# A DiT backbone on one core: the modulation's products change sides on TensorE

## What is computed

```python
def adaln_params(cond, w, b):
    mod = (jax.nn.silu(cond) @ w + b)[:, None, :]
    return jnp.split(mod, 6, axis=-1)
...
sh1, sc1, g1, sh2, sc2, g2 = adaln_params(c, ada_w[i], ada_b[i])
a = rms_norm(h, norm_g[i, 0]) * (1.0 + sc1) + sh1
```

## Time and profile before

| | |
|---|---|
| median of 3 runs | 3562.78 us (3562.68 to 3563.37) |
| the profiled execution | 3563.18 us |
| its span, first to last instruction | 3561.2 us |
| granted TensorE clock, mean | 0.91 |
| PE busy | 3002.9 us (84%) |
| DVE busy | 2108.3 us (59%) |

### The profile page before, as it was taken

How to read it: one execution, slowest core, us unless ns; L and a number is a source line. 1 busy time by engine, 2 the same in 40 slices (tenths; PEclk the granted TensorE clock), 3 DMA queues, 4 the chain that set the end, 5 groups by cost and what they waited for, 6 DMA issues and landing times.

```text
span 3561.2 us, 53031 instructions
## 1 busy us (share of the span) xinstructions
PE 3002.9 (84%) x20336; PEld 2752.0 (77%) x20336; DVE 2108.3 (59%) x2904; ACT 1211.9 (34%) x1744; POOL 140.0 (4%) x176
## 2 busy tenths in 40 slices
PE   7994882775998998899997768989875998989996
PEld 4772761664998998898997666767675998989996
DVE  3996998456535555645655246656446555664655
ACT  3113112333323243223341335656433333432332
POOL 0000000000000000000000001222100000000000
PEclk9996986887999999999998689999997999999998
DMA  6441430110222121122221110000021222223222
GB/s 239 170 142 45 132 106 12 42 48 30 77 71 71 65 77 65 60 71 71 71 89 57 38 48 25 1 1 1 24 71 41 89 89 78 95 78 106 91 93 77
DMA packets 69270, 254.28 MB, mean 71 GB/s; under 512 B 6672, under 2 KB 6928, under 8 KB 67984
## 3 DMA queue, kind: packets, MB, share of 16 engines
q1 hardware_dynamic: 54976, 202.60, 16.8%
q0 software_dynamic: 10880, 41.95, 3.6%
q10 hardware_dynamic: 3280, 7.86, 0.6%
HBM read 248.19 MB, written 4.19 MB: 71 GB/s over the span
## 4 chain that ended last, share of the span: by engine, by line
PE 65%; DVE 18%; issue 9%; ACT 7%; DVEq 1%; DMA 1%; POOL 0%; SPq 0%; ACTq 0%
PE PS L1165 54%; PE PS L1346 4%; DVE c L924 2%; PE PS L1333 2%; DVE w_lo L758 2%; DVE dw_acc L927 2%; DVE t L764 2%; DVE h L843 1%; DVE rms L768 1%; PE PS L1319 1%; PE PS L1174 1%; ACT t L427 1%; ACT a_hi L454 1%; PE PS L1320 1%; ACT prob L739 1%
## 5 line engine op out<-in xcount | busy, mean ns | idle before, releaser
L1165 PE MATMUL PS<-a_hi,w_hi 128*128 128x320 f32 (+4 forms) x4032 | 914.8, 309 | 245.6 <-DVE a_lo L802 157.5
L1165 PE MATMUL PS<-a_lo,w_hi 128*128 128x320 f32 (+4 forms) x4032 | 901.3, 306 | 0.0
L1165 PE MATMUL PS<-a_hi,w_lo 128*128 128x320 f32 (+4 forms) x4032 | 896.3, 305 | 0.0
L1165 PEld LDWEIGHTS PS<-a_hi,w_hi 128*128 128x128 f32 x4032 | 684.0, 198 | 261.9 <-DVE a_lo L802 163.1
L1165 PEld LDWEIGHTS PS<-a_lo,w_hi 128*128 128x128 f32 x4032 | 685.4, 198 | 0.0
L1165 PEld LDWEIGHTS PS<-a_hi,w_lo 128*128 128x128 f32 x4032 | 682.7, 198 | 0.0
L758 DVE TENSOR_TENSOR w_lo<-raw,w_hi 128x1024 fp32r<-128x1024 f32 x364 | 442.2, 1220 | 390.1 <-ACT w_hi L413 383.8
L413 ACT ACTIVATE w_hi<-raw 128x1024 fp32r<-128x1024 f32 x364 | 382.0, 1050 | 2.7 <-DVE y L1036 1.4
L1165 PE MATMUL PS<-z_hi,w_hi 128*128 128x320 f32 (+1 forms) x1408 | 309.1, 301 | 22.3 <-DVE z_lo L969 15.7
L1165 PE MATMUL PS<-z_lo,w_hi 128*128 128x320 f32 (+1 forms) x1408 | 304.7, 298 | 0.0
L1165 PE MATMUL PS<-z_hi,w_lo 128*128 128x320 f32 (+1 forms) x1408 | 304.3, 298 | 0.0
(11 more groups left out here) (160 smaller groups left out, 3525.0 us busy)
## 6 DMA issues: line engine op xcount, KB each, us to landing
raw<-wstream SPq DMA_DIRECT2D x364, 512.0 KB, 3.3
z<-adastream POOLq DMA_DIRECT2D x24, 1024.0 KB, 6.2
c<-adastream POOLq DMA_DIRECT2D x16, 1024.0 KB, 7.9
ada_first<-adastream SPq DMA_DIRECT2D x4, 2048.0 KB, 20.2
h<-xT SPq DMA_DIRECT2D x1, 2560.0 KB, 15.0
h<-xT ACTq DMA_DIRECT2D x1, 2560.0 KB, 11.9
out<-h ACTq DMA_DIRECT2D x1, 2048.0 KB, 9.5
out<-h ACTq DMA_DIRECT2D x2, 1024.0 KB, 4.3
```

The costliest lines, as they stand in the source:

```text
L1165: last = MM(PS[:, 2 * j + m, 0:n], wt[:, j, k, :], mv[:, k, m * n:(m + 1) * n], start=(k == 0 and p_ == 0), stop=(k == tiles - 1 and p_ == 2))
```

## The change

The operands change sides. A 128 x 128 block of the modulation's weights is now the stationary operand and `silu_c[:, k, :]` (128 x 2) the moving one; eight such matmuls sum straight into the 128 x 2 columns in PSUM that the turns used to write. The rows in PSUM, the copies of them by ACT, the tile `ada_row` and the turns go, with the semaphores `row_ready` and `ada_turned`. A group is 16 matmuls of the program. The sums move from PSUM bank 5 to bank 6. DVE's addition of the bias waits for `ada_used` in place of `ada_turned`.

```diff
-            return PS[:, 5, ds(512 - 4 * N_MOD + 2 * tile, 2 * n)]
+            return PS[:, 6, ds(512 - 4 * N_MOD + 2 * tile, 2 * n)]
...
-            def ada_rows_out(g):
-
-                act.wait_ge(ada_used, g + 1)
-                if above_zero(g - 1):
-                    act.wait_ge(ada_turned, g - 1)
-                A(ada_row[:, g % 2], PS[0:2, 6 + g % 2, 0:2 * P], ACT.Copy).then_inc(row_ready, 1)
...
-                        for r in range(x["ada_per"]):
-                            g = x["ada"] + x["ada_per"] * i + r
-                            act.wait_ge(ada_used, g + 1)
-                            act.wait_ge(ada_turned, g - 1 if r else g)
-                            A(ada_row[:, r % 2], PS[0:2, 6 + r % 2, 0:2 * P], ACT.Copy).then_inc(row_ready, 1)
...
-                dve.wait_ge(ada_turned, x["used"])
+                dve.wait_ge(ada_used, x["used"])
...
-            def ada_rows(g, weights, b):
-
-                for k in range(KT):
-                    last = MM(PS[0:2, 6 + b, 0:2 * P], silu_c[:, k, :], weights[:, k, :], start=(k == 0), stop=(k == KT - 1))
+            def ada_columns(g, weights):
+
+                for r in range(2):
+                    for k in range(KT):
+                        last = MM(ada_sums(2 * g + r, 1), weights[:, k, r * P:(r + 1) * P], silu_c[:, k, :],
+                                  start=(k == 0), stop=(k == KT - 1))
                 last.then_inc(ada_used, 1)
-
-            def ada_turn(g, b):
-
-                pe.wait_ge(row_ready, g + 1)
-                for r in range(2):
-                    last = MM(ada_sums(2 * g + r, 1), ada_row[:, b, r * P:(r + 1) * P], ident[0:2, 0:2], start=True, stop=True)
-                last.then_inc(ada_turned, 1)
...
-                        if above_zero(g - 1):
-                            pe.wait_ge(row_ready, g - 1)
-                        ada_rows(g, ada_first[:, g], g % 2)
-                        if g == ADA_FIRST // 2:
-                            pe.wait_ge(norm_step, x["pre"]["s"] + 6)
-                        if g:
-                            ada_turn(g - 1, (g - 1) % 2)
+                        ada_columns(g, ada_first[:, g])
                         if g == ADA_FIRST // 2 - 1:
                             average(x["pre"]["s"] + 4, wide_ap(x["pre"]["t"], x["pre"]["w"])[:, 0], x["pre"]["w"])
-                    ada_turn(ADA_FIRST - 1, (ADA_FIRST - 1) % 2)
...
-                            if r > 1:
-                                pe.wait_ge(row_ready, g - 1)
-                            ada_rows(g, slot_r, r % 2)
-                            if r:
-                                ada_turn(g - 1, (r - 1) % 2)
-                        ada_turn(x["ada"] + x["ada_per"] * (i + 1) - 1, (x["ada_per"] - 1) % 2)
+                            ada_columns(g, slot_r)
```

More of the change, by code:

```diff
@@ L200, in backbone @@
         dw_acc = sb("dw_acc", [P, CC - 640 + PAD], F32, rF + 2 * 2592)
-        ada_row = sb("ada_row", [2, 2, 2 * P], F32, rF + 2 * 2592 + 2688)
-        assert (CC - 640 + PAD) * 4 <= 2688 and 2 * 2592 + 2688 + 2048 <= 4 * 2592
+        assert (CC - 640 + PAD) * 4 <= 2 * 2592
         raw = sb("raw", [P, 2, KT, P], F32, rW)
@@ L253, in backbone @@
         ada_used, mod_ready, cond_ready = sem("ada_used"), sem("mod_ready"), sem("cond_ready")
-        row_ready, ada_turned = sem("row_ready"), sem("ada_turned")
         const_loaded, rope_loaded = sem("const_loaded"), sem("rope_loaded")
@@ L502, in _ @@
                 if kind == "pre":
-                    if "mod" in x:
-                        ada_rows_out(0)
                     pre_squares(x)
-                    if "mod" in x:
-                        for g in range(1, ADA_FIRST // 2):
-                            ada_rows_out(g)
                     root(s + 5, w)
                     if "mod" in x:
[L511 to L515, removed]
+                        split(0, 0)
+                        split(0, 1)
                         act.dma_start(h[:, :, 640:TOK], xT[:, :, 640:TOK]).then_inc(h_loaded[1], 16)
```

## The result

The changed kernel takes 3620.35 us (median of 4 runs, 3609.09 to 3621.34) against 3562.73: 57.6 us more, a ratio of 1.0159 with a 95% interval of 1.0142 to 1.0177. The profiled execution is the fastest of the four, 3609.09 us; the other three lie within 1.0 us of each other at 3620 to 3621.

A forecast was written before the change was run, and what follows sets the result against it. It took TensorE's modulation groups to bound the start and DVE both stages; 19.3 us in the start, 42 in stage A and 0 in stage B, on the profiled 3563.2, gave 3624 us in the median, range 3600 to 3646.

The forecast's parts named there:

- The bounds of before: Stages: DVE bounds both, at 27.54 us a pair in A (TensorE 26.76) and 29.06 in B (TensorE busy 23.98).
- The price of a record: Modulation groups: a 128-column load with its two-column matmul costs 0.111 us at full clock, 0.2135 at half.
- The rival in which a record costs 0.111 at either clock: Whole kernel: the clock falls but loads don't slow; start gains 3 us, 3560, not slower; chance 0.03.
- The clock: TensorE: never rises in the start; in stage A falls 3.8 us behind the units, needs 5.0 to return.
- The rival that it holds under loads: Whole kernel: loads keep the clock up, start gains at most 3.8 us, 3559, not slower; chance 0.07.
- The start: Eight groups at 6.83 us put DVE's addition of the bias at 68.5 instead of 49.17, 19.3 us later.
- Stage A: TensorE's pair takes 33.5 us against DVE's 27.54 and becomes the bound; seven times 6.0, 42 us.
- Two cases of the earlier trace: Full clock held 1.9 or 5.4 us behind wide matmuls; used to bound stage A's loss at 28 to 58 us.
- Stage B: TensorE's pair takes 26.7 us, under DVE's 29.06, so DVE stays the bound and the loss is 0.
- The sum: Whole kernel: 19.3 + 42 = 61.3 us on the profiled 3563.2, 3624 in the median.
- the signs named ahead: Trace: clock 0.50 to some 87 us, records 0.21 apart, units 33 to 34 apart, seven DVE waits of some 6 us.

The follow-up runs named there:

- the two parts of the stages: Kernel before with the operands swapped only in stage A: 3597.95 us against 3559.22; only in stage B: 3557.84 against 3559.34.
- the run in which 28 of 96 records a pair were worth all of the loss: Kernel before with stage A alone swapped, each pair's third group multiplying one of eight input tiles (sums incomplete): 3559.96 us against 3559.34.
- the wide forms: Changed kernel with the moving operand repeated to 128, 96, 64 or 32 columns: 3554.50 (again 3556.51), 3556.48, 3568.94 and 3604.33 us.
- the two profiles: Changed kernel, nothing altered, profiled in its first measurement (3609.1 us) and in a repeat on another chip (3616.4 us; median 3616.88 against 3558.67).

## Why the prediction was right

- **The bounds of before.** DVE in both stages, with TensorE 0.8 us behind in A: shown by the two parts of the stages (38.7 us in A, none in B) and by the run in which 28 of 96 records a pair were worth all of the loss.
- **The price of a record.** 0.2135 at half clock was taken from the 128-column records around those of the earlier trace rows (the 0.43 us shown there would give 0.215); measured 0.213. 0.111 at full clock was taken from the turns' loads of two rows; measured 0.112 with two moving columns and 0.111 with 128. The rival in which a record costs 0.111 at either clock (3560) is out. What the Trainium skill says in "TensorE: Matmul & The Clock Gate", section "LDWEIGHTS (loading the stationary operand)", a load's columns over 1.2 GHz, an estimated 107 ns for 128, fits the full clock alone; at half clock a record with its load takes 0.213 us, twice that, and the measurement decides.
- **The clock.** It stayed low for the whole start and fell in every pair of stage A. The rival that it holds under loads (3559) is refuted by the changed kernel, and the wide forms show the other side, that with the same loads and more moving columns it does hold. The Trainium skill's page "TensorE: Matmul & The Clock Gate", section "What's actually happening", says that the gate goes by how busy the engine has been. The busy time of the profile is not what it goes by here: from 100.50 to 116.30 loads and matmuls are both busy for 15.80 of 15.80 us at a clock of 0.50, and what parts the runs is the number of moving columns.
- **The start.** 19.3 us were forecast, 18.5 measured; 0.55 of the difference is that the first weights landed at 10.79 in place of 11.34.
- **Stage A.** 42 us were forecast from 3.8 us of full clock behind the units and 5.0 us to come back; 34.0 and 40.7 were measured in the two profiles. In the first the clock held 4.3 us on average and came back after 4.0, so the pair was 32.5 us in place of the 33.5 of the sum. Two cases of the earlier trace rows, 1.9 and 5.4 us, were taken as the bounds, and the falls lay between them, 2.3 to 5.5 us. The sum took one mean pair; the true ones are of two lengths, near 31.6 and 34.7, and how many of each an execution has makes its time. That the usual execution comes within 2 us of the 42 is in part luck: the sum had no term for it.
- **Stage B.** Nothing, as forecast: the lag is 1.3 us less behind it than ahead of it in the trace, and the run of it alone is 1.5 us under before, inside the interval.
- **The sum.** 61.3 us and 3624 were forecast, 57.6 and 3620.35 measured. The 5 us that the first profile gives back behind stage B had no term, and by the estimate above they are not part of the usual execution.
- Of the signs named ahead, one was badly chosen: the column of the granted clock shows 1.00 in the start, because no change is on record there. The distance of the records was the sign that could be read. Two came out in kind and not in size: the units start 31.6 or 34.7 us apart, none of them 33 to 34, and DVE's seven added waits are (49.4 - 17.6)/7 = 4.5 us on average in place of 6.

What stays open: why the time of before falls into two groups some 5 us apart, and whether the 5 us behind stage B are the same; why the clock falls early in some pairs with two columns and in none with 32; and what raised it in the middle of the start in one execution with 64.

## What to carry to other kernels

The form of the product that made TensorE load all the time and move two columns a load was paid twice here: by its own records at half clock (0.213 us in place of 0.112), and by the units behind it until the clock was back. TensorE's busy time said nothing of it. So when operands change sides, compare the moving columns of the two forms and read the distance of the records, and look for which engine bounds each stage: the same columns cost 39 us in one and none in the other. If such loads can't be avoided, try a repeated moving operand: with 128 columns it cost nothing beside the load and won back 60 us.

## What the runs showed of the hardware

- The same program on the same data can find the clock up or down: with 64 moving columns it rose in the middle of the start in one profiled execution and not in two others, some 10 us apart in the time of the kernel.
- With 96 moving float32 columns it rose from the low clock as it did with 128 (at 17.0 and 16.5 us). In stage A it held with 64, but for two short falls, and with 32 it fell in every pair.
- With 2 columns it stayed at half through 27.44 and 27.30 us of back-to-back loads and matmuls in the start.
- A matmul of 128 float32 columns behind a load of 128 columns costs what one of 2 columns does at full clock, 0.111 us against 0.112.
